# A decoder layer on one core: the past values taken in pairs of sequences with a fourth buffer, and four instruction moves around them

## What is computed

```python
# decoder_layer(x, c, past_k, past_v, past_up, p)
mod = jnp.dot(jax.nn.silu(c), p['w_ada']) + p['b_ada']
h = x * (1 + scale1) + shift1
proj = jnp.dot(h, p['w_in'])                       # q, k, v, u_a, v_a
attn = moba_attention(q, k_all, v_all, pos0, p['rel_bias'])
#   logits = q . k + bias; prob = softmax(logits); out = prob @ v     (per head, per sequence)
gm = chunk_spatial_gate(gelu(u_a), layer_norm(gelu(v_a)), p['w_s'], p['b_s'])
mixed = concat([rms_norm(gm, p['norm_a_g']), rms_norm(attn, p['norm_b_g'])])
x = layer_norm(ALPHA * x + gate1 * jnp.dot(mixed, p['w_out']), ...)
h = x * (1 + scale2) + shift2
up = jnp.dot(h, p['w_up'])                         # then a causal convolution of width 3 over its rows
ff = jnp.dot(silu(a) * b, p['w_down'])
y = layer_norm(ALPHA * x + gate2 * ff, ...)
```

## Time and profile before

| what | value |
|---|---|
| median of 3 runs | 1399.15 us (1396.6, 1399.15, 1401.26) |
| the profiled execution's own time | 1399.97 us |
| its span in the profile | 1398.3 us |
| PE busy | 1372.2 us (98%) |
| DVE, ACT, POOL busy | 836.8, 570.3, 104.8 us |
| mean DMA rate over the span | 232 GB/s |
| mean granted clock of PE | 0.995 of full speed |

### The profile page before, as it was taken

One profiled execution on the slowest core, in us unless ns is written; L12 is line 12 of the kernel. 1 busy time (PEld: TensorE's weight loads), 2 busy tenths in 40 slices (PEclk: granted clock), 3 DMA queues, 4 the chain that ended last, 5 costly groups with the idle time before them and its releaser, 6 DMA issues.

```text
span 1398.3 us, 29220 instructions
## 1 busy us (share of the span) xinstructions
PE 1372.2 (98%) x11397; PEld 1297.5 (93%) x11397; DVE 836.8 (60%) x1404; ACT 570.3 (41%) x847; POOL 104.8 (7%) x250
## 2 busy tenths in 40 slices
PE   7999999999999999999999999999999999999996
PEld 6998888999788888999999999999999999999996
DVE  3475556568875468565576454675665544766755
ACT  4533222354642326543444333444444333444533
POOL 1000000004121000010010000110110000100000
PEclk9999999999999999999999999999999999999999
DMA  9999998975887988775545544445445544454441
GB/s 372 409 342 389 338 337 311 354 261 181 298 311 277 359 303 318 291 291 197 184 150 177 169 161 162 161 147 181 164 155 176 163 167 160 146 181 163 172 151 68
DMA packets 89907, 324.94 MB, mean 232 GB/s; under 512 B 10653, under 2 KB 10653, under 8 KB 89440
## 3 DMA queue, kind: packets, MB, share of 16 engines
q1 hardware_dynamic: 82512, 297.34, 59.4%
q0 software_dynamic: 6880, 24.10, 5.1%
q10 hardware_dynamic: 432, 2.33, 0.4%
HBM read 318.05 MB, written 5.67 MB: 232 GB/s over the span
## 4 chain that ended last, share of the span: by engine, by line
PE 93%; DMA 3%; DVE 2%; ACT 1%; issue 0%; SPq 0%; DVEq 0%; ACTq 0%; POOLq 0%
PE ps L451 28%; PE ps L453 28%; PE ps L452 27%; PE ps L467 6%; DMA raw<-w_in 1%; PE ps L794 1%; DMA adaY<-w_ada 1%; DMA KV<-values 1%; DMA ada<-w_ada 1%; PE ps L658 1%; PE ps L480 0%; DVE wL L1433 0%; PE ps L708 0%; PE ps L580 0%; DVE xT L1878 0%
## 5 line engine op out<-in xcount | busy, mean ns | idle before, releaser
L1433 DVE TENSOR_TENSOR wL<-raw,wH 128x1024 fp32r<-128x1024 f32 x372 | 449.4, 1219 | 354.6 <-ACT wH L1029 351.7
L1029 ACT ACTIVATE wH<-raw 128x1024 fp32r<-128x1024 f32 x372 | 389.4, 1053 | 586.6 <-PE ps L453 557.5
L451 PE MATMUL ps<-hL,wH 128*128 128x288 f32 x2016 | 602.1, 299 | 2.8 <-ACT U L1339 1.9
L453 PE MATMUL ps<-hH,wH 128*128 128x288 f32 x2016 | 599.5, 297 | 0.0
L452 PE MATMUL ps<-hH,wL 128*128 128x288 f32 x2016 | 596.7, 296 | 0.0
L451 PEld LDWEIGHTS ps<-hL,wH 128*128 128x128 f32 x2016 | 379.4, 188 | 18.3 <-issue 13.2
L452 PEld LDWEIGHTS ps<-hH,wL 128*128 128x128 f32 x2016 | 380.2, 189 | 0.5 <-issue 0.5
L453 PEld LDWEIGHTS ps<-hH,wH 128*128 128x128 f32 x2016 | 378.7, 188 | 0.0
L451 PE MATMUL ps<-ffL,wH 128*128 128x288 f32 x688 | 204.6, 297 | 0.0
L452 PE MATMUL ps<-ffH,wL 128*128 128x288 f32 x688 | 203.0, 295 | 0.0
L453 PE MATMUL ps<-ffH,wH 128*128 128x288 f32 x688 | 202.4, 294 | 0.0
(11 more groups left out here) (256 smaller groups left out, 1005.5 us busy)
## 6 DMA issues: line engine op xcount, KB each, us to landing
raw<-w_up SPq DMA_DIRECT2D x168, 512.0 KB, 3.6
ada<-w_ada SPq DMA_DIRECT2D x112, 512.0 KB, 6.1
raw<-w_down SPq DMA_DIRECT2D x83, 512.0 KB, 3.5
raw<-w_in SPq DMA_DIRECT2D x80, 512.0 KB, 7.3
adaX<-w_ada SPq DMA_DIRECT2D x40, 512.0 KB, 5.2
adaY<-w_ada SPq DMA_DIRECT2D x40, 512.0 KB, 6.9
raw<-w_out SPq DMA_DIRECT2D x32, 512.0 KB, 5.7
KV<-keys POOLq DMA_DIRECT2D x16, 512.0 KB, 5.6
```

The lines of the kernel that those rows point to most:

```text
L451: nc.tensor.matmul(out, wH[:, w:w + P], rhs_lo(kk), start=start, stop=False)
L453: mm = nc.tensor.matmul(out, wH[:, w:w + P], rhs_hi(kk), start=False, stop=stop)
L1029: nc.scalar.activation(wH[:, o:o + cols], raw[:, o:o + cols], ACT.Copy).then_inc(hi_done, 1)
L1433: vec_tt(wL[:, o:o + cols], raw[:, o:o + cols], wH[:, o:o + cols].bitcast(F32), ALU.subtract).then_inc(split_done, 1)
```

## The change

Six edits, on all engines but SP. (1) A fourth buffer `KV3` is laid over `Vrm`. Values go round four buffers, so the transfer of values 3 waits for the release of `attend(7)`'s bank on ACT (`released(pool, ("PV", HEADS - 1))`), and later ones wait for the value step four before, not three before. (2) POOL reads both page numbers before it waits. (3) PE takes values 2 and 3, and 4 and 5, one right after the other, each pair behind two output slabs. (4) ACT does a one-column `Exp` before it copies the second half of the values out of PSUM, and `copy_turned(1)` stands ahead of `exponentials(2)`. (5) ACT does `up_rows` ahead of the wait and copy of the `ada` sums, in the first up phase. (6) DVE masks the queries of sequence 0 ahead of the normalisation of the gating group.

```diff
--- before.py
+++ after.py
@@ -296,7 +296,8 @@
         ps = ctx.enter_context(nc.psum_tensor("ps", [P, 8, 512], F32))
         bias_rows = nc.dram_tensor("bias_rows", [2 * HEADS, REL_N], F32, kind="Internal").ap()
         ident = cst[:, C_ID:C_ID + P]
-        KV = (KV0, KV1, KV2)
+        KV3, _ = place("KV3", [P, 2048], over=o_v)
+        KV = (KV0, KV1, KV2, KV3)
 
         def sem(name):
             return ctx.enter_context(nc.semaphore(name))
@@ -324,7 +325,7 @@
         var_ready, va_sd, va_rs, va_ready, gm_ready = sem("var_ready"), sem("va_sd"), sem("va_rs"), sem("va_ready"), sem("gm_ready")
         vas_done = sem("vas_done")
         logit_ready, exp_ready, prob_ready = sem("logit_ready"), sem("exp_ready"), sem("prob_ready")
-        kv_in, kv_used = [sem("kv_in0"), sem("kv_in1"), sem("kv_in2")], sem("kv_used")
+        kv_in, kv_used = [sem("kv_in0"), sem("kv_in1"), sem("kv_in2"), sem("kv_in3")], sem("kv_used")
         qm_ready, ptm_ready, pages_in, tails_stored = sem("qm_ready"), sem("ptm_ready"), sem("pages_in"), sem("tails_stored")
         s_logit, s_exp, s_prob = sem("s_logit"), sem("s_exp"), sem("s_prob")
         sq_part, sq_ready, m_ready, mH_ready, m_split = (
@@ -698,8 +699,8 @@
 
             def past_values(n):
 
-                buf = n % 3
-                pe.wait_ge(kv_in[buf], 32 * ((4, 4, 0)[buf] + n // 3 + 1))
+                buf = n % 4
+                pe.wait_ge(kv_in[buf], 32 * ((4, 4, 0, 0)[buf] + n // 4 + 1))
                 pe.wait_ge(ptm_ready, n + 1)
                 for kt in range(2):
                     for h in range(HEADS):
@@ -752,12 +753,12 @@
             pe.wait_ge(sq_part, HEADS)
             sum_squares("sum b", 4, 3, [tile(proj, k, 0, SEQ) for k in (8, 14, 15)], 0, SEQ)
             out_slab(9)
+            out_slab(10)
             past_values(2)
-            out_slab(10)
             past_values(3)
             out_slab(11)
+            out_slab(12)
             past_values(4)
-            out_slab(12)
             past_values(5)
             out_slab(13)
             past_values(6)
@@ -1164,6 +1165,7 @@
                 act.wait_ge(v_stored, 16)
                 for k in range(4):
                     mix_hi_at(k)
+                nc.scalar.activation(small[:, 153:154], eps_col(0), ACT.Exp)
                 copy_v(0, 1)
                 copy_v(1, 1)
                 copy_v(2, 1)
@@ -1175,10 +1177,12 @@
                 exponentials(1)
                 act.wait_ge(k_stored, 16)
                 for h in range(2, HEADS):
-                    if h > 2:
+                    if h > 3:
                         copy_turned(h - 2)
                     out_step(h - 1)
                     attended(h - 2)
+                    if h == 2:
+                        copy_turned(1)
                     exponentials(h)
                 copy_turned(HEADS - 2)
                 out_step(7)
@@ -1353,11 +1357,11 @@
                     for u in range(2):
                         for i in range(1, 17):
                             half = i // 8 - 1
+                            if i % 8 == 0:
+                                up_rows(u * 2 + half, ("up", 0, "ab"[half]), u, u * 16 + (s0 + i - 1), u * 6 + (td + 3 * half))
                             if i == 16:
                                 filled(act, ("turn up", u - 1) if u else ("turn", U_SC2B))
                                 ada_copy(u * 16 + (A_UP + 16))
-                            if i % 8 == 0:
-                                up_rows(u * 2 + half, ("up", 0, "ab"[half]), u, u * 16 + (s0 + i - 1), u * 6 + (td + 3 * half))
                             if u or i > 5:
                                 hi_ahead(u * 16 + s0, u * 4 + s0 // 4, i)
                             if i % 8 == 0:
@@ -1706,12 +1710,12 @@
                 x = tiles(xT, 2 * g, 2, SEQ, ROWS)
                 steps.link(vec_tt(x, x, tiles(S4, 0, 2, SEQ, ROWS), ALU.add))
 
+            for p in range(6, 10):
+                in_done(dve, p)
+            own_queries(0)
             norm_prompt(0, 0)
             invert_root(0, "sum ad", SEQ)
             norm_samples(0).then_inc(m_ready, 1)
-            for p in range(6, 10):
-                in_done(dve, p)
-            own_queries(0)
             for k in range(4):
                 mix_lo_at(k)
             dve.wait_ge(table_in, TABLES * 16)
@@ -2109,15 +2113,17 @@
             def load_kv(idx, parts=range(PAGES)):
 
                 n, name = idx % NSEQ, "keys" if idx < NSEQ else "values"
-                buf = n % 2 if idx < NSEQ else n % 3
+                buf = n % 2 if idx < NSEQ else n % 4
+                page_of = [pool.value_load(pages[0:1, n * PAGES + pg:n * PAGES + pg + 1], min_val=0, max_val=n_phys - 1) for pg in parts]
                 if idx == NSEQ + 2:
                     pool.wait_ge(logit_ready, HEADS)
-                elif idx > NSEQ + 2:
-                    pool.wait_ge(kv_used, idx - 2)
+                elif idx == NSEQ + 3:
+                    released(pool, ("PV", HEADS - 1))
+                elif idx > NSEQ + 3:
+                    pool.wait_ge(kv_used, idx - 3)
                 elif idx >= 2:
                     pool.wait_ge(kv_used, idx - 1)
-                for pg in parts:
-                    page = pool.value_load(pages[0:1, n * PAGES + pg:n * PAGES + pg + 1], min_val=0, max_val=n_phys - 1)
+                for pg, page in zip(parts, page_of):
                     pool.dma_start(KV[buf][:, pg * 1024:(pg + 1) * 1024],
                                    io[name][bass.ds(page, 1), :, :].rearrange("a p c -> (a p) c")).then_inc(kv_in[buf], 16)
 
```

## The result

| | before | after |
|---|---|---|
| median, runs side by side | 1400.54 us (1396.6 to 1402.92, 7 runs) | 1396.52 us (1393.7 to 1396.85, 7 runs) |
| the profiled execution's own time | 1399.97 us | 1395.35 us |
| its span | 1398.3 us | 1393.7 us |
| PE busy | 1372.2 us | 1372.4 us |

The ratio is 0.9972 (95% interval 0.996 to 0.9985): the change gains 4.0 us, where the forecast was 8.3 from the profiled execution and 9.3 from these runs' median. The sign was right, the size was twice what is there. The time lies in the range given, near its upper end of 1397.0; but that end was set by a rival that did not happen (the last values still late), so lying inside it is no merit of the sum.

A forecast was written before the change was run, and what follows sets the result against it. PE was taken as the bound, busy 1372.2 of 1398.3 us. Gains 5.4 + 0.7 - 0.1 + 1.9 + 0.4 + 0 = 8.3 us gave a forecast of 1391.2 us; 8-in-10 range 1388.5 to 1397.0, the sum's own 1389.8 to 1393.5.

The forecast's parts named there:

- the last values still late: Transfers held by DMA engines, not by their issue, so PE's wait for values 7 stays: 1396.3 us, chance 0.10.
- Values 7 in time: Main term, values 6 to first transpose: PE's wait and the slow clock behind it go, 11.21 to 5.8 us, gain 5.4.
- the first rival: The slow stretch behind the wait for values 7 is not fully in timed runs: gain 5.1, 1394.1 us, chance 0.12.
- Is the transfer in time?: Check on values 7: both pages issued by 417.2 us, landed by 425.8, needed by PE at about 429.
- The third rival: Values 7 still land late, held by the DMA engines; only the other terms, 2.9 us, stay: 1396.3 us, chance 0.10.
- The fourth, late values 3: Values 3, waiting for `attend(7)`, land late; two such PE waits make the kernel slower: 1401.6 us, chance 0.06.
- Pairs: Past values: two newly made pairs of slabs and value steps gain 0.66 us, less 0.1 for lost cover of DVE.
- the second rival: DVE becomes the bound between slabs in a row (10 and 12); 2 to 3 us come back: 1393.7 us, chance 0.10.
- The copies to `U`: First up phase, around the `ada` bursts: both PE waits for ACT's copies go, 1.9 us gained.
- `copy_turned(1)`: Early attention: PE's wait for ACT's copy of the turned probabilities goes, 0.4 us gained, 0 at worst.
- Masked queries and Exp: First attention steps, two waits of 0.5 us each: counted as 0, from 0.9 gained to 0.4 lost.

The follow-up runs named there:

- the second profile of before: The kernel before, unchanged, profiled once more in a single execution: 1400.63 us.
- values only: The kernel before with only the fourth buffer, the page numbers read ahead and the pairs: 1397.24 us, ratio 0.9984.

## Why the prediction was right or wrong

**Values 7 in time, 5.4 us: the step that failed.** The mechanism was right (the wait, the slow clock behind it, and that both go), the size was not. The sum took 2.2 us of wait and 3.2 of slow clock from one execution and counted both as there in every one. In five profiles the wait has 0.45 to 2.2 us at this place, and the slow clock lasts 6.8 us in one of them, 3.4 in one, and is absent in three. Against the second profile of before, the way from values 6 to the transpose is shorter by 7.75 - 5.75 = 2.0 us, and that is what the term is worth in a run without the slow clock. Such runs are the majority, at most 63 of 87, and the slowed ones lift the median of before by only 0.5 us (1398.9 against 1398.4). That is the first rival, which had 0.12, with a shorter wait besides (1.8 us, not 2.2). The evidence against it, that the median lay within 1 us of the profiled execution, was weak: that execution had no slow loop, which hid up to 3.6 us, and so looked ordinary while it carried 3.5 us too much in one place and too little in another. The rule cited there, from the Trainium skill's page "TensorE: Matmul & The Clock Gate", "Part 1: The HAM clock gate (the 'warmup' mystery)", that the number of slow matmuls differs between runs of one kernel, agrees with these runs (6.8, 3.4 and no us at 0.50 behind nearly the same wait).

**Is the transfer in time?** Yes, but my 417.2 us for the last issue was wrong. POOL issues values 6 first and reads the pages of 7 after that; the last issue came at 419.6, 2.4 us later. With 8.6 us it landed at 428.2, for a need at 428.88 + 0.94 = 429.8. Where a landing took 10.4 us, in values only, PE waited 0.15. The third rival came this near: the issue moved forward by 3.9 us and not by more than six. The fourth, late values 3, shows nowhere: no profile with four buffers has a wait for them.

**Pairs, 0.66 less 0.1.** From the input stage's end to the start of values 6 it takes 428.50 - 346.34 = 82.16 us in the kernel without the edits in attention, in place of 82.67 and 82.65: 0.5 gained, forecast 0.56. A double slab and its pair take 423.62 - 414.99 = 8.63, not 8.47. No wait for DVE stands at slab 10 or 12, so the second rival fell.

**The copies to `U`, 1.9.** Right: 0.95 and 1.0 us in the profiles, 0.19% in its own runs (interval 0.01 to 0.37%).

**`copy_turned(1)`, 0.4.** 0.16 us by the profiles (87.91 - 87.75). The wait of 0.42 us went, and one of 0.22 for DVE came at the next output slab.

**Masked queries and Exp, 0 from -0.4 to 0.9.** -0.18 together, inside the range and for the reason given, that ACT arrives later (0.73 us and not 0.5). I had weighed that delay only against the table load; it also delays the copy of `Vn`, whose bank PE wants.

**The sum.** In the usual run it is 90.40 - 87.93 = 2.5 us to the first transpose and 1.95 at `U`: 4.4 us, and 0.9969 to 0.9972 is 3.9 to 4.3. The 8.3 us come near only against an execution with the long slow stretch: 93.88 - 87.93 + 1.95 = 7.9. The range of the sum itself was also too narrow by its own ends. They were 4.8 for values 7, -0.3 for the pairs (0.7 less 1.0), 0 for `U`, 0 for `copy_turned(1)` and -0.4 for the two last, 4.1 together. With 5.4 for values 7 and 1.0 for `U` the prediction had 5.7; by its ends the slow case would have been 1395.1 and not 1393.5. The pace of the loops adds 0 to 3.6 us to either kernel and is noise of the comparison: 768, 1536 and 960 matmuls at 1.1 ns each. It hides the slow stretch in a single time: the two profiled executions of before took 1399.97 and 1400.63 us, one with the slow stretch and fast loops, the other the reverse.

## What to carry to other kernels

Before a term is priced from a stretch of slow clock, ask whether the stretch is in every execution: a second profile, or the mean clock of each timed run, answers it. A profile whose time is near the median may still be unusual in two places that cancel. An instruction put into an engine's idle time is free only if nothing ahead of it moves later at the same time: two edits with a gain each (0.55 and 0.08 us) lost 0.18 together.

## What was not expected of the hardware

- PE has two paces at a granted clock of 1.00: with 128x128 weights and 288 columns, 133.3 or 134.4 ns from start to start, kept for up to 206 us (the 1536 matmuls of the longest loop), with nothing found on the other engines to tell them apart. Written out as straight code, the second and third phase had the fast pace 8 times in 8; as loops they had it 7 times in 26. What sets it is open.
- A wait of PE of 2.03 or 2.22 us was followed by 3.4 and 6.8 us at a granted clock of 0.50, one of 1.79 or 1.80 us by none. With a wait of 5.82 us the clock falls before the wait ends: a mean of 0.70 in 434 to 436 us, with PE's work back at 436.25.
- A 512 KB transfer issued 0.9 us earlier landed no earlier (9.5 us in place of 8.6), and the same transfer at the same place took 6.8 to 9.5 us in five executions.
